# Bias rows and indexer scores in fewer passes, attention three slots later, and odd convolution taps summed by accumulating DMAs

## The reference, cut to what matters

```
proj = h @ w_in                                    # u_glu, q, k, v, qi, ki, wi, gates
u = a * sigmoid(gt);  u = sum_j w_dw[j] * u[t - 30 + j] + b_dw          # 31 taps
y_conv = silu(layer_norm(u)) @ w_conv_out
score[q,s] = sum_h relu(qi[q,h] . ki[s]) * wi[q,h] / 32                 # indexer, 16 heads of 64
sel = top 64 of the admissible score               # per block of 128 queries
y_attn = softmax(q . k[sel] / 8) v[sel] @ w_attn_out                    # 16 heads of 64
...
bias[h, q, s] = rel_bias_2[bucket(q - s), h]       # second block, 8 heads
```

## Time and profile before

| | us |
|---|---|
| median of 3 runs | 2697.97 (2696.64 to 2699.96) |
| the profiled execution | 2699.8 |
| its span, from the first to the last instruction | 2698.0 |
| PE busy | 2584.3 (96%) |
| DVE busy | 1684.5 (62%) |
| ACT busy | 1286.2 (48%) |

### The profile page before, as it was taken

One profiled execution on the slowest core, in us unless ns is written; L12 is line 12 of the kernel. 1 busy time (PEld: TensorE's weight loads), 2 busy tenths in 40 slices (PEclk: granted clock), 3 DMA queues, 4 the chain that ended last, 5 costly groups with the idle time before them and its releaser, 6 DMA issues.

```text
span 2698.0 us, 28994 instructions
## 1 busy us (share of the span) xinstructions
PE 2584.3 (96%) x11660; PEld 2111.5 (78%) x11660; DVE 1684.5 (62%) x1914; ACT 1286.2 (48%) x1797; POOL 3.4 (0%) x10
## 2 busy tenths in 40 slices
PE   4999989999989999999999899999999999999998
PEld 3777767877868888888888787778788888888886
DVE  6899788988875555555555544666554454445455
ACT  4535666755454444444444454544454444444443
POOL 0000000000000000000000000000000000000000
PEclk9999999999989999999999999999999999999999
DMA  9888445777855556665554554345455555555553
GB/s 352 326 332 324 157 156 197 270 281 278 342 222 203 218 204 234 241 242 212 209 205 176 180 186 158 141 156 187 172 177 195 187 195 197 188 194 194 188 187 125
DMA packets 80566, 579.29 MB, mean 215 GB/s; under 512 B 8964, under 2 KB 8964, under 8 KB 10544
## 3 DMA queue, kind: packets, MB, share of 16 engines
q1 hardware_dynamic: 78480, 564.82, 57.8%
q10 hardware_dynamic: 1440, 9.81, 0.9%
q0 software_dynamic: 512, 2.81, 0.3%
HBM read 573.73 MB, written 3.67 MB: 214 GB/s over the span
## 4 chain that ended last, share of the span: by engine, by line
PE 76%; DVE 7%; ACT 3%; issue 1%; DMA 0%; ACTq 0%; DVEq 0%; SPq 0%
PE bank L640 72%; DVE wlo L1459 2%; PE bank L604 1%; ACT whi L965 1%; DVE raw L1469 1%; DVE X L1454 1%; DVE cv L1664 1%; ACT PR L965 0%; DVE SS L1454 0%; DVE cv L1454 0%; PE bank L752 0%; PE bank L800 0%; ACT SS L1335 0%; DMA raw<-in_w_in 0%; PE bank L885 0%
## 5 line engine op out<-in xcount | busy, mean ns | idle before, releaser
L1459 DVE TENSOR_TENSOR wlo<-raw,whi 128x1024 fp32r<-128x1024 f32 x882 | 1077.3, 1224 | 957.1 <-ACT whi L965 953.4
L965 ACT ACTIVATE whi<-raw 128x1024 fp32r<-128x1024 f32 x882 | 932.3, 1059 | 1289.2 <-PE bank L640 1169.2
L640 PE MATMUL bank<-whi,HTh 128*128 128x512 f32 x2560 | 706.2, 398 | 8.8 <-ACT HTh L965 5.8
L640 PE MATMUL bank<-wlo,HTh 128*128 128x512 f32 x2560 | 687.6, 391 | 3.5 <-DVE wlo L1459 3.5
L640 PE MATMUL bank<-whi,HTl 128*128 128x512 f32 x2560 | 689.2, 391 | 0.5 <-DVE HTl L1775 0.5
L640 PEld LDWEIGHTS bank<-wlo,HTh 128*128 128x128 f32 x2560 | 481.6, 188 | 106.4 <-DVE wlo L1459 4.8
L640 PEld LDWEIGHTS bank<-whi,HTl 128*128 128x128 f32 x2560 | 483.5, 189 | 103.7 <-DVE HTl L1775 1.0
L640 PEld LDWEIGHTS bank<-whi,HTh 128*128 128x128 f32 x2560 | 472.5, 189 | 113.9 <-issue 15.6
L1469 DVE CUSTOM_DVE_ANT_0 raw<-raw,GT,VECS 128x2048 f32<-128x2048 f32 x96 | 225.0, 2347 | 0.2 <-DMA raw<-in_w_ada 0.2
L640 PE MATMUL bank<-whi,ACTh 128*128 128x512 f32 x704 | 191.6, 394 | 0.0
L640 PE MATMUL bank<-wlo,ACTh 128*128 128x512 f32 x704 | 190.0, 392 | 0.0
(11 more groups left out here) (217 smaller groups left out, 1235.5 us busy)
## 6 DMA issues: line engine op xcount, KB each, us to landing
raw<-in_w_in SPq DMA_DIRECT2D x128, 1024.0 KB, 4.9
raw<-in_w_ada SPq DMA_DIRECT2D x96, 1024.0 KB, 6.5
raw<-in_w_gate SPq DMA_DIRECT2D x88, 1024.0 KB, 4.8
raw<-in_w_up SPq DMA_DIRECT2D x88, 1024.0 KB, 4.8
raw<-in_w_down SPq DMA_DIRECT2D x88, 1024.0 KB, 4.8
raw<-in_w_o SPq DMA_DIRECT2D x16, 1024.0 KB, 7.0
raw<-in_w_out SPq DMA_DIRECT2D x16, 1024.0 KB, 4.8
raw<-in_w_attn_out SPq DMA_DIRECT2D x8, 1024.0 KB, 4.8
```

Of the source, the lines that this page charges most:

```text
L640: i = e.matmul(bank[2 * ch.st + t][:, :], (xl if ps == 1 else xh)[:, k, tk(t)], (lo if ps == 2 else hi)[:, j * 512:j * 512 + 512], start=c ...
L965: return e.activation(dst, src, ACT.Copy, scale=scale)
L1459: e.tensor_tensor(lo, src, r32(hi), S_).then_inc(lo_done, 1)
```

## The change

Four things are changed. **Bias rows:** `RB` now holds the 33 biases of 8 heads once, so that one matmul gives all 8 rows on 8 partitions, one copy takes them to `RD[0:8]`, a small DMA takes them to DRAM (`biases`), and a second one spreads them over the 128 rows of `scratch`; it waits for piece 81. **Scores:** in each slot two heads are made for both query blocks; the two heads lie in different halves of the partitions (0 to 63 and 64 to 127) and go to different banks, where before the two heads of a block lay in the same half and went to one bank. One ACT instruction takes the relu of all four. **Attention** begins at slot 99 in place of 96, and "OT" comes two slots after "PV", so that a group takes 9 slots. **Convolution:** of the first 20 taps, tap 0 is as before, the odd ones are multiplied by ACT and added to `cv` by a DMA from GpSimd that accumulates, the even ones are done by DVE alone; from tap 20 on all is as before.

```diff
-    ATT0 = M["kiwi"] + 16
+    ATT0 = M["kiwi"] + 19
-    ON_ACT = [j % 4 != 3 for j in R(KW)]
+    BY = ["first"] + [("dve", "dma")[j % 2] if j < 20 else ("act", "dve")[j % 4 == 3] for j in R(1, KW)]
+    def tap_done(j, hf):
+        if BY[j] == "first":
+            return cv_mul(0, hf, 3)
+        if BY[j] == "dma":
+            return cv_add[hf], 16 * BY[:j + 1].count("dma")
+        return cv_dve(j, hf, 0 if BY[j] == "act" else 3)
...
         def bias_rows():
-            for h in R(8):
-                ...
-                e.matmul(bank[5][:, 0:384], RB[0:33, h, :], OH[0:33, :], start=True, stop=True).then_inc(*rb_pe.one(h))
-                yield 1
+            w.wait_ge(*xt_act(14))
+            e.matmul(bank[5][0:8, 0:384], RB[0:33, :], OH[0:33, :], start=True, stop=True).then_inc(*rb_pe.one("rows"))
+            yield 1
...
             for hp in R(8):
-                half = hp % 2
                 if hp:
-                    w.wait_ge(*sel_act[t](hp - 1))
-                for r in R(2):
-                    h = 4 * (hp // 2) + 2 * r + half
-                    i = e.matmul(b[:, r * 256:r * 256 + nk], qiT[64 * half:64 * half + 64, h // 2, tk(t)],
-                                 kiT[64 * half:64 * half + 64, 0:nk], start=True, stop=True)
+                    w.wait_ge(*sel_act(hp - 1))
+                for t in (1, 0):
+                    nk = 128 * (t + 1)
+                    for r in R(2):
+                        i = e.matmul(bank[6 + r][:, 256 - 256 * t:256 - 256 * t + nk], qiT[64 * r:64 * r + 64, hp, tk(t)],
+                                     kiT[64 * r:64 * r + 64, 0:nk], start=True, stop=True)
...
+                e.activation(rel[hp % 2][:, :, 0:384], both[:, :, 0:384], ACT.Relu, scale=1.0 / 32).then_inc(
+                    *sel_act.one(hp))
...
         def attend(t):                              # PE; ACT and DVE alike
                 i.then_inc(*att_pe[t].one("PV", g))
-                yield 1
+                yield 2
                 w.wait_ge(*att_dve[t]("norm", g))
                 transposes(bs[0], stg[2 + 2 * t], 2).then_inc(*att_pe[t].one("OT", g))
...
             for n, (j, hf) in enumerate(TAPS[2:]):  # DVE
-                if ON_ACT[j]:
+                if BY[j] == "act":
                     w.wait_ge(*cv_mul(j, hf, 3))
...
-                else:
-                    conv_before(j, hf)
+                elif BY[j] == "dve":
+                    w.wait_ge(*tap_done(j - 1, hf))
                     for i in R(4):
...
-        w.wait_ge(*rb_act(7))                       # GpSimd
-        e.dma_start(A["scratch"], RD[:, :, :]).then_inc(scr_in, 16)
+        w.wait_ge(*rb_act("rows"))
+        e.dma_start(A["biases"], RD[0:8, :]).then_inc(rd_out, 16)
+        w.wait_ge(rd_out, 16)
+        w.wait_ge(pe_done, M["k1"])
+        e.dma_start(A["scratch"].rearrange("p h i -> p (h i)"),
+                    A["biases"].rearrange("h i -> (h i)").partition_broadcast(128)).then_inc(scr_in, 16)
+        for j, hf in TAPS:
+            if BY[j] == "dma":
+                w.wait_ge(*cv_mul(j, hf, 3))
+                w.wait_ge(*tap_done(j - 1, hf))
+                e.dma_start(cv[:, 4 * hf:4 * hf + 4, :], PR[hf][:, :, :], accum_op=ALU.add).then_inc(cv_add[hf], 16)
```

More of the change, by code:

```diff
@@ L291, in build @@
     MK = at("MK", 69632, [2, T])
-    RB = at("RB", 41984, [8, 128])
-    RD = at("RD", 50176, [8, 384])
+    RB = at("RB", 41984, [8])
+    RD = at("RD", 50176, [384])
     O2 = at("O2", 66560, [2, 1024])
@@ L298, in build @@
     PART = [at(f"PART{i}", o, [2, 512]) for i, o in enumerate([32768, 0, 4096, 8192, 12288, 46080])]
+    rel = [at(f"rel{i}", 75776 + 4096 * i, [2, 512]) for i in range(2)]
     stg = [at(f"stg{i}", 75776 + 2048 * i, [512]) for i in range(6)]
@@ L311, in build @@
     assert P0 + 75776 + 2048 * 6 <= nc.sbuf_usable_end
-    bank = [nc.alloc_psum_tensor(f"bank{i}", [128, 512], f32) for i in range(8)]
+    bank = [nc.alloc_psum_tensor(f"bank{i}", [128, 512], f32) for i in range(6)]
+    both = nc.alloc_psum_tensor("bank67", [128, 2, 512], f32)
+    bank += [both[:, 0, :], both[:, 1, :]]
     spare = [0]
@@ L348, in build @@
     raw_in = [S(f"raw{i}_in") for i in range(NRAW)]
-    vec_in, c_in, row_in, rb_in, scr_in, bt_in, out_done = [
-        S(n) for n in ("vec_in", "c_in", "row_in", "rb_in", "scr_in", "bt_in", "out_done")]
+    vec_in, c_in, row_in, rb_in, rd_out, scr_in, bt_in, out_done = [
+        S(n) for n in ("vec_in", "c_in", "row_in", "rb_in", "rd_out", "scr_in", "bt_in", "out_done")]
     x_in = [S(f"x{i}_in") for i in range(2)]
+    cv_add = [S(f"cv_add{hf}") for hf in range(2)]
     hi_done, lo_done, pe_done, pe_t0 = [S(n) for n in ("hi_done", "lo_done", "pe_done", "pe_t0")]
@@ L369, in build @@
     fh_act = steps("fh_act", list(R(16)))
-    rb_pe = steps("rb_pe", list(R(8)))
-    rb_act = steps("rb_act", list(R(8)))
+    rb_pe = steps("rb_pe", ["rows"])
+    rb_act = steps("rb_act", ["rows"])
     u_act = steps("u_act", [(j, t) for j in R(2) for t in R(2)])
@@ L377, in build @@
     two_dve = steps("two_dve", [0, 1])
-    sel_pe = [steps(f"sel{t}_pe", list(R(8))) for t in R(2)]
-    sel_act = [steps(f"sel{t}_act", list(R(8))) for t in R(2)]
+    sel_pe = steps("sel_pe", list(R(8)))
+    sel_act = steps("sel_act", list(R(8)))
     sel_dve = [steps(f"sel{t}_dve", [("s", hp, r) for hp in R(8) for r in R(2)] + ["outside"]
@@ L1102, in bias_rows @@
         def bias_rows():
[L1103 to L1106, removed]
+            w.wait_ge(*rb_pe("rows"))
+            copy(RD[0:8, :], bank[5][0:8, 0:384]).then_inc(*rb_act.one("rows"))
+            yield 1
         def u_tanh(j, t):
@@ L1127, in t_job, with select @@
             yield 1
-        def select(t):
-            nk = 128 * (t + 1)
-            b = bank[6 + (t == 0)]
+        def select():
             for hp in R(8):
-                sg = stg[t + 2 * (hp % 2)]
-                w.wait_ge(*sel_pe[t](hp))
+                w.wait_ge(*sel_pe(hp))
                 if hp >= 2:
-                    w.wait_ge(*sel_dve[t]("s", hp - 2, 1))
-                e.activation(tri(sg[:, :], 2)[:, :, 0:nk], tri(b[:, :], 2)[:, :, 0:nk], ACT.Relu,
-                             scale=1.0 / 32).then_inc(*sel_act[t].one(hp))
+                    for t in R(2):
+                        w.wait_ge(*sel_dve[t]("s", hp - 2, 1))
+                e.activation(rel[hp % 2][:, :, 0:384], both[:, :, 0:384], ACT.Relu, scale=1.0 / 32).then_inc(
+                    *sel_act.one(hp))
                 yield 1
@@ L1168, in conv_products @@
             w.wait_ge(*cv_dve("pad"))
-            w.wait_ge(*rb_pe(7))
+            w.wait_ge(*rb_pe("rows"))
             w.wait_ge(*pro_dve("lam1"))
             for n, (j, hf) in enumerate(TAPS):
-                if ON_ACT[j]:
-                    if j:
-                        before = j - 1 if ON_ACT[j - 1] else j - 2
-                        if before > 0:
-                            w.wait_ge(*cv_dve(before, hf, 0))
+                if BY[j] != "dve":
+                    if j > 1:
+                        w.wait_ge(*tap_done(max(i for i in R(j) if BY[i] != "dve"), hf))
                     for i in R(4):
```

52 lines of the change are left out of this document (21 added, 31 removed).

## The result

The changed kernel takes 2680.05 us in the median of 4 runs (2672.73 to 2683.28) against 2698.64 us (2696.64 to 2699.96, 4 runs) for the kernel before on the same chip: ratio 0.9928, 95% interval 0.9906 to 0.995, so 18.6 us less. That is faster by more than 0.2%, inside the range, and 6 us above the 2674 that was predicted. The executions of the changed kernel lie over 10.6 us, those of before over 3.3.

What follows compares the result with a forecast made beforehand. PE, busy 96% of the time, was taken to bound the kernel. Terms of -7.5, -5.3, -6.5, -6.8, +0.5 and +1 sum to -24.6 us, from 2699.8 to 2675.2, as a median 2674; range 2666 to 2695.

Steps and rivals of the forecast that it cites:

- Mask and first group: Start of the attention: piece 99 no longer waits, one wait of about 2.5 us stays; -6.5 us, bounds -3.2 and -9.
- OT: Attention's transposes: a piece more before them removes PE's waits for the normalized tile; -6.8 us, bound -4.
- first addition: Convolution: the first addition by DMA stands behind the write of `scratch` and may be late; +0.5 us, bounds 0 and 4.
- tail: Last additions (tap 19) fall where ACT wants their buffer for tap 20, some 8 us on; +1 us, bounds 0 and 3.
- Bias rows: First stage: seven of eight bias matmuls go, each 1.08 us of PE's slot; -7.5 us, bounds -4 and -8.6.
- Scores: Score slots: eight rows take 0.85 us instead of 1.51, in eight slots; -5.3 us, bounds 0 and -6.
- no stretch at half clock there: Sign for the changed profile: about piece 98, one wait for `wlo` of 2 to 3 us and no half clock.
- bound of -3.2: Low end of the mask and first group term, if the clock falls as before and costs half of 6.61 us.
- steady additions hidden: Convolution: additions by DMA after the first fit their room, at its tightest 11.2 us, and cost 0.
- price of 8.4 us: Time taken for one accumulating DMA of 512 KB, from the nearest row by bytes, 1536 KB from GpSimd.
- rival of the slow additions: Convolution: additions landing late hold DVE and `wlo`, so the kernel ends slower, above 2703 us; chance 0.13.
- that of the feeders: PE's work shrinks, but weights in the first stage and DVE among scores set the pace: 2684 to 2692; chance 0.17.

Runs made afterwards that it cites:

- quick execution: The profiled execution of the changed kernel, the quickest of its first four: 2672.73 us.
- again: The changed kernel repeated without an edit: 2680.11 us, ratio 0.9925; its profiled execution took 2680.36 us.
- bias_only: The kernel before with the bias rows of the change alone: 2690.97 us, ratio 0.997.
- bias_scores: The changed kernel with attention and taps as before, so only bias rows and scores changed: 2686.9 us, ratio 0.9957.
- same_half: The changed kernel with a slot's four score matmuls in the order half 0, half 0, half 1, half 1: 2678.26 us, ratio 0.9919.
- after: The changed kernel's own profile, taken in its first group of runs: that execution took 2672.73 us.
- no_att: The changed kernel with the whole attention as before (start at slot 96, OT one slot after PV, eight slots a group): 2682.57 us, ratio 0.9938.
- no_dma: The changed kernel with the taps as before the change, without additions by DMA: 2677.09 us, ratio 0.9918.
- tap6: The changed kernel with tap 6 given to the accumulating DMA too: 2673.87 us, ratio 0.991.
- t19: The changed kernel with tap 19 added by DVE again in place of the DMA: 2677.2 us, ratio 0.9917.
- tap6_19: The changed kernel with tap 6 added by DMA and tap 19 by DVE: 2673.49 us, ratio 0.9905.
- tap6_att16: The changed kernel with tap 6 by DMA and the attention begun at slot 96 again: 2677.07 us, ratio 0.9921.

## Why the prediction was right, and where its sizes were off

**The whole.** From PE's end of piece 95 to that of piece 145, the stretch of the attention, the kernel before takes 181.9 us, the quick execution 170.0 and "again" 176.7. The four terms of this stretch (mask, "OT", first addition, tail) summed to 11.8 us; the quick execution has 11.9 of them, "again" 5.2.

**Bias rows: right.** Predicted 7.5 us; in the profiled execution PE ends piece 32 at 138.5 us for 146.0. Of these 7.5 us, 0.9 are there at piece 23 (112.0 for 112.9), ahead of the rows; counted from there it is 6.6 by piece 32 and 8.1 by piece 60. In bias_only the medians give 8.0.

**Scores: right.** Predicted 5.3. From the end of piece 83 to that of piece 91 PE takes 31.0 us (289.5 to 320.5) for 36.0 (298.5 to 334.5): 5.0. The medians of bias_scores and bias_only give 13.0 - 8.0 = 5.0. DVE did not set the pace: PE has no wait from 289 to 335 us. Nor does the order inside the slot matter (same_half). Whether two halves would do it with one bank, no run shows, since before both heads had one half and one bank.

**Mask and first group: the mechanism right, the size for the usual execution not.** Piece 99 no longer waits and one wait of 2.83 us stays, as written. But "no stretch at half clock there" holds in two of the three profiled executions of the changed kernel (after and same_half). In "again" the clock falls behind this wait; the logits and the four matmuls behind them take 345.54 - 343.53 + 1.51 = 3.52 us where the quick execution takes 2.09 (343.23 to 345.32 by its timeline), so that some 1.4 us more are lost. The bound of -3.2 was made for this case, and the likeliest value should have lain nearer to it: a wait of 2.83 us was left standing, where before the clock had fallen at 358.65, 0.7 us behind the waits for `wlo` of 0.80 and 2.41. The prediction puts that fall behind all three waits; the one of 3.69 us lies inside it (359.48 to 363.17), so the two for `wlo` were enough.

**"OT": right that the wait goes, wrong that it is the extra slot's to take.** The term was priced with the taps of before. Either the taps by DMA (no_att: 2.4 us left of 6.7) or the attention's move as a whole (no_dma: none left) takes most of this wait, so it can't be paid for twice. The 2 by 2 table of gains points the same way: neither 13.0 (bias_scores), the attention's move alone 21.8 (no_dma), the DMAs alone 17.3 (no_att), both 18.8 and 21.6 (again, same_half). Alone they are worth 8.8 and 4.3 us, together 5.8 to 8.6. The profiled executions do not: 2685.50 - 2677.06 = 8.4 and 2685.50 - 2681.36 = 4.1 alone, together 12.8 and 12.3 in after and same_half, and 5.1 in "again". So what the medians lack is at least in part the falls and the tail, and how much is the shared wait stays open.

**Convolution: steady additions hidden, as predicted.** DVE waits for one addition only, 2.8 us, and PE does not see it. The price of 8.4 us was near: median 7.0, from 4.5 to 13.1 where 5 to 11 was the sign; the slowest is the second addition, behind the write of `scratch`. So the rival of the slow additions did not come about: none took 16. Nor did that of the feeders, with pieces 2.72 us apart and scores at 0.85.

**The tail: the step that was mis-sized.** It was put at +1 us with bounds 0 and 3, with ACT's buffer for tap 20 named as the place. It is 0 in the quick execution, where PE waits for nothing there. In "again" it is the wait of 2.82 us and half of 3.4 us, 4.5 in all, outside its bounds; PE's ends of pieces show it, 1.8 us behind the quick execution at piece 131 (463.7 for 461.9) and 6.4 at piece 137 (486.3 for 479.9). Two things were wrong. The room was put at some 8 us, and ACT leaves 6.6 and 5.4, less than the 8.4 us that the prediction itself takes for an addition; so a wait of ACT is no rare case: it has one for tap 19 in tap6 (1.84 and 1.29 us) and in same_half (0.52) too. And the clock's fall behind PE's wait had been left out.

These two places, 1.4 and 4.5 us, are most of the 7.6 us between the quick execution and "again". That they are also the 6 us between forecast and median is likely, not shown: of the changed kernel three executions were profiled, and the loss at the tail stands in one of them. t19 and tap6 were to take one place each away. tap6 gained 5 to 6 us in the medians, and in its profile the wait at piece 98 is shorter and no fall follows it, which speaks for the first; but that profile is of its quickest execution, only 2672.73 - 2671.48 = 1.3 us ahead of the quick execution. t19's gain is 3.6 us better than that of "again", little more than the 2.8 by which repeats of one kernel differ. So both places are shown in the traces, and their prices in the medians stay open.

**A version that beats both.** Tap 6 by DMA (tap6 and tap6_19): the eight executions lie between 2671.48 and 2677.16, median 2673.50; the thirteen of the changed kernel (its own, again, same_half) between 2672.73 and 2683.28, median 2678.80. Seven of the eight are under 2675.3, and three of the thirteen. That is about 5 us more, and 25 to 26 us under the kernel before. The groups were timed beside the kernel before, whose medians lie within 1.3 us of each other (2698.64 to 2699.91).

## What to carry to other kernels

Two remedies for one wait can't both be paid with it: price the second with the first in place, and undo both, not only each, to see it. A wait that stays just as long as one behind which the clock fell is not paid with its own length alone; shorten it. Here it went from 2.83 to 1.28 us by moving the one tap that shared its slots, and behind waits of 1.28, 1.23 and 1.15 us there (tap6, tap6_19, tap6_att16) no fall came right behind them in the one execution profiled of each. A DMA that replaces an engine's addition also holds its source buffer until it lands, so look for who wants to write that buffer next, not only for who wants the sum, and compare its room with the price of the DMA: here 5.4 to 6.6 us with 8.4.

## What the runs showed of the hardware

**Matmuls in different halves of the partitions ran side by side, and out of the order of the program.** Starts (ns from the first of the slot) of the eight records of a slot of scores, by width, read from single records of the traces:

```
before      0   213   325   436   548   766   982  1199
widths    128   128   128   128   256   256   256   256
changed     0     7   320   327   536   543   645   652
widths    256   256   256   256   128   128   128   128
same_half   0    14   321   334   537   550   646   659
widths    256   256   256   256   128   128   128   128
```

In same_half the program has both matmuls of half 0 (256, 128) ahead of those of half 1 (256, 128), and yet the records pair 256 with 256 and 128 with 128, 13 or 14 ns apart: half 1 did not wait for half 0. The Trainium skill ("TensorE: Matmul & The Clock Gate", "The mechanism") has matmuls of different row groups overlap, about 4 ns apart; the trace agrees on the overlap, with 7 and 13 to 14 ns. It also calls matmuls a strict FIFO in start and end, which the starts of same_half do not bear out.

**The same wait, with and without a fall of the clock.** 2.83 us at 339.26 (after) and 2.86 at 339.64 (same_half) had full clock behind them, 2.86 at 339.42 (again) 3.4 us at half. So it is not the wait's length that decides between them; what does is left open here.

**An addition by DMA took 4.5 to 13.1 us for the same 512 KB** in one execution, and in the same place of two executions 5.8 and 10.3. The weights' issues around it stand at the same distances in both, but the weights landed later too: from 440 to 470 us the median from issue to landing of the units of `w_in` is 6.2 us in the quick execution and 8.3 in "again". So it is not the additions alone that were slow there; the cause stays open.
